# Attention softmax: the second map's scaling moved from VectorE to GpSimd, and 32 small products at the beginning

## The reference, cut to what matters

```python
def gqa_block(qb, k, v):
    s = jnp.einsum('bqhgd,bshd->bhgqs', qb, k).astype(jnp.float32) * (HEAD_DIM ** -0.5)
    p = jax.nn.softmax(s, axis=-1).astype(v.dtype)
    return jnp.einsum('bhgqs,bshd->bqhgd', p, v)

def diff_block(qb, k, v, lam):
    s = jnp.einsum('bqhmd,bshmd->bhmqs', qb, k).astype(jnp.float32) * (HEAD_DIM ** -0.5)
    p = jax.nn.softmax(s, axis=-1)
    a = p[:, :, 0] - lam[None, :, None, None] * p[:, :, 1]
    return jnp.einsum('bhqs,bshe->bqhe', a.astype(v.dtype), v)

def trunk_layer(x, mod, g_attn, g_ffn, mix_w, moe_w, rope, ctx, lam_init):
    shift1, scale1, gate1, shift2, scale2, gate2 = jnp.split(mod, 6, axis=-1)
    h = rms_norm(x, g_attn) * (1.0 + scale1) + shift1
    m, own_ctx = token_mixing(h, mix_w, rope, ctx, lam_init)
    x = x + gate1 * m
    h = rms_norm(x, g_ffn) * (1.0 + scale2) + shift2
    x = x + gate2 * expert_choice_ffn(h, *moe_w)
    return x, own_ctx
```

## Time and profile before

| | us |
|---|---|
| median of 3 runs (1146.23 to 1149.08) | 1146.9 |
| the profiled execution | 1145.81 |
| its span, first to last instruction | 1144.0 |
| TensorE busy (share of the span) | 1097.6 (96%) |
| VectorE busy | 528.1 (46%) |
| ScalarE busy | 363.2 (32%) |
| GpSimd busy | 132.4 (12%) |

### The profile page before, as it was taken

One profiled execution on the slowest core, in us unless ns is written; L12 is line 12 of the kernel. 1 busy time (PEld: TensorE's weight loads), 2 busy tenths in 40 slices (PEclk: granted clock), 3 DMA queues, 4 the chain that ended last, 5 costly groups with the idle time before them and its releaser, 6 DMA issues.

```text
span 1144.0 us, 28118 instructions
## 1 busy us (share of the span) xinstructions
PE 1097.6 (96%) x12524; PEld 828.2 (72%) x12524; DVE 528.1 (46%) x961; ACT 363.2 (32%) x846; POOL 132.4 (12%) x173
## 2 busy tenths in 40 slices
PE   6999999999999999999998999999999999999993
PEld 4679875666677777777877877777777777777761
DVE  4574538879958142334976033332233223333235
ACT  4333327778753223022163221222222222211103
POOL 2332300000000000002012111111110111110021
PEclk9999999999999999999999999999999999999997
DMA  9932242111031545359987999999999999999993
GB/s 359 299 107 68 77 84 63 35 31 41 1 109 38 184 147 147 106 190 300 355 303 320 402 398 406 407 405 409 414 406 405 408 404 408 405 408 405 410 321 143
DMA packets 86747, 295.32 MB, mean 258 GB/s; under 512 B 27249, under 2 KB 28530, under 8 KB 62050
## 3 DMA queue, kind: packets, MB, share of 16 engines
q1 hardware_dynamic: 79104, 269.77, 61.5%
q0 software_dynamic: 6528, 20.10, 6.1%
q10 hardware_dynamic: 994, 3.65, 0.9%
HBM read 273.25 MB, written 15.00 MB: 252 GB/s over the span
## 4 chain that ended last, share of the span: by engine, by line
PE 85%; DMA 7%; issue 2%; ACT 2%; DVE 2%; SPq 1%; POOLq 0%; POOL 0%; ACTq 0%; DVEq 0%
PE ps L1207 39%; PE ps L772 10%; PE ps L774 9%; PE ps L773 9%; PE ps L994 4%; PE ps L1013 3%; PE ps L1032 2%; PE ps L1036 2%; DMA x_dram<-y_row,rows_t 2%; DMA x_dram<-xn_p 1%; DMA raw_first<-in_w_in_dram 1%; DMA x_f<-x_dram 1%; PE ps L794 1%; DMA raw<-in_w_in_dram 1%; PE ps L978 1%
## 5 line engine op out<-in xcount | busy, mean ns | idle before, releaser
L2124 DVE SCALAR_TENSOR_TENSOR y_row<-ps,gates,gate_q 32x256 f32<-32x256 f32 (+1 forms) x184 | 88.3, 480 | 238.5 <-PE ps L1207 236.0
L1564 ACT ACTIVATE h_t<-ps 128x256 f32<-128x256 f32 x48 | 15.0, 384 | 374.7 <-PE ps L1207 374.7
L772 PE MATMUL ps<-w_hi,ht 128*128 128x512 f32 (+1 forms) x320 | 124.2, 388 | 0.6 <-DVE q_n L1728 0.6
L774 PE MATMUL ps<-w_hi,ht 128*128 128x512 f32 (+1 forms) x320 | 121.8, 381 | 0.0
L773 PE MATMUL ps<-raw_lo,ht 128*128 128x512 f32 (+1 forms) x320 | 121.7, 380 | 0.0
L1207 PE MATMUL ps<-late,xe 128*32 128x256 f32 x1824 | 103.6, 379 | 0.0
L537 DVE TENSOR_TENSOR raw_lo<-raw,w_hi 128x1024 fp32r<-128x1024 f32 x48 | 58.2, 1234 | 78.9 <-ACT w_hi L532 78.2
L1207 PEld LDWEIGHTS ps<-late,xe 128*32 128x32 f32 x1824 | 77.0, 110 | 23.3
L1207 PE MATMUL ps<-raw,xe 128*32 128x256 f32 x1392 | 88.1, 379 | 0.9 <-issue 0.8
L532 ACT ACTIVATE w_hi<-raw 128x1024 fp32r<-128x1024 f32 x48 | 48.7, 1053 | 123.6 <-DMA raw<-in_w_in_dram 68.1
L2354 POOL DMA_INDIRECT xg<-x_dram,rows x48 | 46.1, 961 | 320.7 <-PE ps L1207 293.2
(11 more groups left out here) (315 smaller groups left out, 1831.0 us busy)
## 6 DMA issues: line engine op xcount, KB each, us to landing
late<-in_w_exp_down_dram SPq DMA_DIRECT2D x25, 1024.0 KB, 20.4
late<-in_w_exp_up_dram SPq DMA_DIRECT2D x21, 1024.0 KB, 28.8
late<-in_w_exp_gate_dram SPq DMA_DIRECT2D x17, 1024.0 KB, 24.7
raw<-in_w_in_dram SPq DMA_DIRECT2D x16, 1024.0 KB, 5.5
raw<-in_w_exp_gate_dram SPq DMA_DIRECT2D x16, 1024.0 KB
raw_gate<-in_w_exp_up_dram SPq DMA_DIRECT2D x14, 1024.0 KB
raw<-in_w_exp_up_dram SPq DMA_DIRECT2D x13, 1024.0 KB
raw_gate<-in_w_exp_down_dram SPq DMA_DIRECT2D x13, 1024.0 KB
```

The lines of the kernel that those rows point to most:

```text
L772: pe.matmul(b, stat_hi(k, tt), hi[:, kk, :], start=first, stop=False)
L774: mm = pe.matmul(b, stat_lo(k, tt), hi[:, kk, :], start=False, stop=last)
L2124: return dve.scalar_tensor_tensor(y_row[n % 2][32 * v:32 * v + count, 256 * q:256 * q + 256], bank(b, o, o + 256, src), gates[src, n % EG, ...
```

## The change

VectorE no longer scales the second map. GpSimd does this for all 40 units, in a loop of its own behind its last transfer for the input projection (`pool.tensor_scalar`, 40 instructions): in a plain unit by the reciprocal and by a column of ones, in a differential unit by the reciprocal and by lambda. It waits for the reciprocal (`s_inv`) and signals `s_second`. VectorE's first-map scaling of plain units stays behind the reciprocal; the merge of differential units (`combine`) now waits for `s_second`, and stands between the two row maxima. TensorE's transposes of a plain unit wait for `s_second` too, as soon as they reach the second map.

At the beginning TensorE gets 32 throw-away calls between the first `spin(8)` and `turn_tokens(0)`: rows 32a to 32a+31 of the identity as weights of 64 columns, over 128 columns, into four PSUM banks.

```diff
--- before.py
+++ after.py
@@ -425,7 +425,7 @@
         s_kc = sem("s_kc"); s_kpair = sem("s_kpair"); s_vc = sem("s_vc"); s_vac = sem("s_vac")
         s_qt = sem("s_qt")
         s_sc = sem("s_sc"); s_max = sem("s_max"); s_exp = sem("s_exp"); 
-        s_nrm = sem("s_nrm"); s_c1 = sem("s_c1"); s_comb = sem("s_comb"); s_ptr = sem("s_ptr")
+        s_nrm = sem("s_nrm"); s_inv = sem("s_inv"); s_second = sem("s_second"); s_comb = sem("s_comb"); s_ptr = sem("s_ptr")
         s_ph = sem("s_ph"); s_pl = sem("s_pl"); s_pv = sem("s_pv"); s_oev = sem("s_oev");
         s_ysq = sem("s_ysq"); s_yms = sem("s_yms"); s_yn = sem("s_yn")
         s_yh = sem("s_yh"); s_yl = sem("s_yl")
@@ -870,6 +870,11 @@
 
             part_chunk(0, 0)
             spin(8)
+            for n in range(4):
+                for a in range(4):
+                    for v in range(2):
+                        pe.matmul(bank(1 + a, 0, P, slice(64 * v, 64 * v + 64)), ident[32 * a:32 * a + 32, 64 * v:64 * v + 64],
+                                  ident[32 * a:32 * a + 32, :], start=True, stop=True)
             turn_tokens(0)
             turn_tokens(1)
             spin(8)
@@ -1006,7 +1011,9 @@
                     if p >= PLAIN:
                         pe.wait_ge(s_comb, i - PLAIN * NT + 1)
                     else:
-                        pe.wait_ge(s_nrm, 2 * i + tiles[-1] // per + 1)
+                        pe.wait_ge(s_nrm, i + 1)
+                        if tiles[-1] >= per:
+                            pe.wait_ge(s_second, i + 1)
                     piece_bank_free(n)
                     for b, x in enumerate(tiles):
                         kt = x % per
@@ -1805,22 +1812,22 @@
             def inverse_sums(i):
                 o = 2 * i % 8
                 dve.wait_ge(s_exp, 2 * i + 2)
-                dve.reciprocal(row_inv[:, o:o + 2], row_sum[:, o:o + 2]).then_inc(s_dve, 1)
-                own()
-
-            def normalise(i):
+                dve.reciprocal(row_inv[:, o:o + 2], row_sum[:, o:o + 2]).then_inc(s_inv, 1)
+
+            def normalise_first(i):
+                p, t = PUS[i]
+                cols, o = KTL * P if t < NTL else P, 2 * i % 8
+                a = prob_row(2 * i)[:, 0:cols]
+                if p < PLAIN:
+                    dve.wait_ge(s_inv, i + 1)
+                    dve.tensor_scalar(a, a, row_inv[:, o:o + 1], None, ALU.mult).then_inc(s_nrm, 1)
+
+            def combine(i):
                 p, t = PUS[i]
                 cols, o = KTL * P if t < NTL else P, 2 * i % 8
                 a, b = prob_row(2 * i)[:, 0:cols], prob_row(2 * i + 1)[:, 0:cols]
-                dve.wait_ge(s_dve, own(0))
-                if p < PLAIN:
-                    dve.tensor_scalar(a, a, row_inv[:, o:o + 1], None, ALU.mult).then_inc(s_nrm, 1)
-                    dve.tensor_scalar(b, b, row_inv[:, o + 1:o + 2], None, ALU.mult).then_inc(s_nrm, 1)
-                else:
-                    g = 2 * HB + p - PLAIN
-                    dve.tensor_scalar(b, b, row_inv[:, o + 1:o + 2], lam[:, g:g + 1], ALU.mult, ALU.mult)\
-                       .then_inc(s_c1, 1)
-                    dve.wait_ge(s_c1, i - PLAIN * NT + 1)
+                if p >= PLAIN:
+                    dve.wait_ge(s_second, i + 1)
                     dve.scalar_tensor_tensor(a, a, row_inv[:, o:o + 1], b, ALU.mult, ALU.subtract).then_inc(s_comb, 1)
 
             def probs_turned(i):
@@ -1838,11 +1845,14 @@
             for i in range(SLOTS):
                 if 1 <= i <= len(PUS):
                     inverse_sums(i - 1)
-                    normalise(i - 1)
+                    normalise_first(i - 1)
                 if 0 <= i - LAG < len(PUS) and i not in QUERY_SLOTS:
                     probs_turned(i - LAG)
                 if i + 1 < len(PUS):
                     row_max(2 * i + 2)
+                if 1 <= i <= len(PUS):
+                    combine(i - 1)
+                if i + 1 < len(PUS):
                     row_max(2 * i + 3)
                 if 0 <= i - LAG < len(PUS) and i in QUERY_SLOTS:
                     probs_turned(i - LAG)
@@ -2295,6 +2305,17 @@
             pool.wait_ge(s_free_a, 3 * NT)
             pool.dma_start(new_diff_v[0, 0].rearrange("p h d -> p (h d)"), vb_n[:, 2 + NTL, :]).then_inc(s_out, 16)
 
+            for i, (p, t) in enumerate(PUS):
+                cols, o = KTL * P if t < NTL else P, 2 * i % 8
+                b = prob_row(2 * i + 1)[:, 0:cols]
+                g = 2 * HB + p - PLAIN
+                pool.wait_ge(s_inv, i + 1)
+                if p < PLAIN:
+                    pool.tensor_scalar(b, b, row_inv[:, o + 1:o + 2], one, ALU.mult, ALU.mult).then_inc(s_second, 1)
+                else:
+                    pool.tensor_scalar(b, b, row_inv[:, o + 1:o + 2], lam[:, g:g + 1], ALU.mult, ALU.mult)\
+                        .then_inc(s_second, 1)
+
             pool.wait_ge(s_kout, 32)
 
             pool.wait_ge(s_half, gemm_half(11, 3) + 1)
```

## The result

| | before | changed |
|---|---|---|
| median, us (6 runs each) | 1146.9 | 1152.4 (1151.4 to 1153.7) |
| ratio to before (95%) | | 1.0046 (1.0036 to 1.0056) |
| the profiled execution, us | 1145.81 | 1152.75 |
| its span | 1144.0 | 1150.9 |
| TensorE, VectorE, GpSimd busy, us | 1097.6, 528.1, 132.4 | 1102.3, 506.0, 175.5 |

The change costs 5.5 us by the medians. The forecast was 6.7. VectorE is relieved of 22 us, GpSimd is given 43, and TensorE shows 5 us more although it computes the same but for the 32 small calls at the beginning (1.2 us): the rest is products spread out by waits. Lines have moved by 5 to 7 (L994 is now L999, L998 L1003, L1013 L1020, L1036 L1043, L1801 L1808, L1824 L1831, L1416 L1423).

The account below looks back on a forecast made before the run. TensorE was taken as the bound; late merges and row maxima in four differential heads cost 1.3, 1.85, 1.85 and 1.7, together 6.7 us, all else 0: 1146.9 + 6.7 = 1153.6 us, range 1147.5 to 1160.

Parts of the forecast that it names:

- VectorE's saving is worth 0: Taking the second map's scaling off VectorE gains 0 us, since TensorE waited for none of these scalings.
- 0.52 us of slack, 0.47 late: Differential slots: 0.52 us of slack hides the second map's softmax; the moved merge makes its PSUM bank 0.47 us late.
- larger slack: Rival: the slack is larger than thought and only context slots pay, 1149 us; 0.18 together with a missed cover.
- 0.15 in the slot with query turns: Second differential slot with query turns: TensorE has more to do (3.97 us), so only 0.15 us of lateness is left.
- 1.2 us at the context tile: Differential half, A being a slot's first score product start: late merge delays the next full slot 1.2 us per head.
- The last head, 1.7: Last differential head, whose slots have no query turns and end in the tail: taken to lose 1.7 us.
- d, the time of a GpSimd scaling: GpSimd's time for 768 columns in a differential slot: taken as 0.95 us, bounded by 0.80 and 1.45.
- The quarrel over ports: VectorE and GpSimd at SBUF: GpSimd waits some 0.5 us in plain slots, covered by the spare slot; cost 0 us.
- The products, 0: Throw-away products at the beginning: 1.0 to 2.6 us, hidden by TensorE's 2.75 us idle time before 50.69; cost 0 us.
- VectorE the real bound: Rival: VectorE's 3.63 us of work a slot bounds the differential half, so the change gains, 1142 us; chance 0.08.
- Slow GpSimd: Rival: from d = 1.7 every merge waits for GpSimd; 1163 us at d = 2.4; 0.12 together with clock falls.
- The clock falls: Rival: new TensorE waits, largest 1.2 us, lower the clock; four falls give 1159 us; 0.12 together with slow GpSimd.

Follow-up runs that it names:

- plain_only: Kernel before, with GpSimd scaling the second map in the 20 plain units alone, old order, no throw-away products: 1146.76 us, ratio 0.9996.
- early_inverse: Changed kernel without throw-away products, merge ahead of both row maxima, reciprocal one slot earlier in the differential half: 1146.33 us, ratio 0.9993.
- split_merge: Kernel before, with only the merge's last third (256 of 768 columns) and the short merges between the row maxima: 1148.61 us, ratio 1.0018.
- early_double: early_inverse with GpSimd scaling each differential unit in two instructions, by the reciprocal and then by lambda: 1147.14 us, ratio 0.9999.
- order_only: Kernel before, with the merge between the two row maxima in the differential half, VectorE still scaling, no throw-away products: 1151.25 us, ratio 1.0040.
- merge_first: Changed kernel without throw-away products, merge ahead of both row maxima, reciprocal left where it was: 1148.89 us, ratio 1.0018.

## Why the prediction came out as it did

The direction and the mechanism held, the size was 6.7 us where 5.5 was measured. Here are the steps of the forecast, one by one:

- **VectorE's saving is worth 0.** Right: plain_only 0.9996, early_inverse 0.9993, the latter with 20 us less work on VectorE (507.9 instead of 528.1).
- **0.52 us of slack, 0.47 late.** Right. The second scores start 1.09 instead of 0.75 behind the first at 271.77, and the two slots are 0.51 longer together. In split_merge the slack takes a delay of 0.40 us at no cost. The rival *larger slack* falls by the wait at 271.77, where the exponent is waited for. Of the 0.51, 0.06 fall in the first of the two slots and 0.45 in the second.
- **0.15 in the slot with query turns.** It doesn't show where I put it: 274.77 to 278.73 is 3.96, as before (3.97). The lateness is there (the product of 278.73 is 1.74 long), but TensorE's next work doesn't pay for it separately; it is swallowed by the wait at the context tile. This term should have been 0.
- **1.2 us at the context tile.** 1.06 measured. The order of the steps was right, and most were a little too long: the reciprocal starts at A + 3.63 (282.36, forecast 3.70), GpSimd at A + 3.89 (4.01), with 0.98 us of its own (0.95), the merge at A + 4.90 (5.02) and the next full slot 0.86 behind its end. The forecast did not see how the cause divides: 0.88 of it comes from the order even without GpSimd, 0.18 from GpSimd.
- **The last head, 1.7.** 1.11 measured (299.26 to 315.77 before, 304.04 to 321.66 now, up to the first product of L1046, now L1053). This is the term I had not worked out but taken. The kernel before already waits there, which fits its having less to lose, though no run tests this: its score products at 305.99 take 1.71 instead of 1.56 us, its context products at 313.41 take 1.07 instead of 0.91, and the first product behind them waits 0.17 for an exponent.
- **The sum.** 0.98 + 1.56 + 1.57 + 1.11 = 5.2 against 1.3 + 1.85 + 1.85 + 1.7 = 6.7. Of the 1.5 too many, 0.6 is the last head and 0.3 each of the others; in a full head that is the query slot's 0.15 and 0.17 at the context tile, less 0.04 that the two slots before cost more.
- **d, the time of a GpSimd scaling.** 0.98 in a differential unit, inside the bounds and near the copy's end of them. The Trainium skill's (GPSIMD Engine Reference, § 4.1 Engine selection) "roughly line-rate" for one input fits that loosely: VectorE takes 0.68 for the same instruction. The estimate of 1.7 us from the two-input figure in § 3.1 Elementwise doesn't fit.
- **The quarrel over ports.** In a plain slot GpSimd's scaling of the same 768 columns takes 1.41 us instead of 0.98. It started 0.06 behind VectorE's, which took 0.62. The column of ones is not the reason: with it and VectorE elsewhere the instruction takes 0.98 to 0.99 (early_double). The rows of one plain slot:

```profile
215.17 0.62 DVE L1823 TENSOR_SCALAR probs<-probs,row_inv 128x768 f32<-128x768 f32 x1
215.23 1.41 POOL L2314 TENSOR_SCALAR probs<-probs,row_inv,tab 128x768 f32<-128x768 f32 x1 [3.85 <-DVE row_inv L1815]
```

  I had expected some 0.5 of waiting, and that it is harmless; plain_only shows both. The beginning shows the other side. Where GpSimd's copy started first, VectorE's subtraction took 1.73 us (changed kernel, 48.91 and 49.58) or 1.74; in order_only VectorE started first (48.52 and 48.84) and took 1.22. That is the Trainium skill's rule (SBUF — State Buffer, § Who interferes with whom) that the first to start keeps the shared ports, and the traces agree.
- **The products, 0.** Their 1.21 us was within the bounds of 1.0 to 2.6. The first product behind the idle time starts at 51.37 instead of 50.69, but the weight chunk that it waits for has landed 0.67 later too (46.58 instead of 45.91), and the idle time is 2.89 us, longer than the 2.75 of the earlier trace rows: TensorE stood waiting at that point all the same. The clock stayed at 1.00 behind that idle time and had fallen to 0.53 in the kernel before, which is one more reason why two single profiles don't give the price.
- **VectorE the real bound.** Not in this change. The 3.63 us of VectorE's work a slot were a real warning, though: with 0.3 us more on top (merge_first) VectorE is the bound.
- **Slow GpSimd.** It didn't happen, and my price for it was wrong. I had given 1163 at d = 2.4, with 4 of the 9.8 us by ordinary slots; 1162 was reached at 2.06, through the context tile and the clock alone. Nor did every merge wait from 1.7 on: at 2.06 GpSimd held up 8 of 20 merges, and TensorE's products waited for 4.
- **The clock falls.** Not in this change: the granted clock is 1.00 in every stretch from 170 to 338 us, and TensorE's longest new wait in the attention is 0.41 us. The 1.2 us that I had taken as the largest new wait come in pieces, the two longest of 0.40 and 0.21 us (283.62 and 284.71).

## What to carry to other kernels

Before an operation is moved to an idle engine, follow the *result* through the queues that it must now pass: here the price came from the place of one 1 us instruction between two that TensorE needs, and not from the slower engine. Work out the slack of each buffer that comes free from one slot's starts (0.52 us here, of a 3.64 us slot). A delay inside it cost nothing here (0.40), one beyond it about the excess (0.51 for a delay of 0.94), and the slots followed by short ones have the least. If work is to be handed to another engine all the same, start its first step as early as its inputs are there (the reciprocal, one slot earlier). With that, even a doubled GpSimd time cost nothing that could be measured.

## What the runs showed of the hardware

- A GpSimd scaling with two per-row scalars takes 0.98 us for 128x768 float32 and 0.45 for 128x128, which makes an estimate of 0.83 ns a column with 0.34 us fixed. It starts 0.26 us after the start of the reciprocal that releases it (282.36 to 282.62).
- A second dependent GpSimd instruction starts 1.08 us after the first of 0.98: 0.10 us between them (early_double, 282.25 and 283.33).
- 64 instructions of 32x64 tiles over 128 columns took 1.21 us together, where 16 of the router's took 0.64.
- The granted clock fell to 0.50 after TensorE had stood 0.3 to 0.7 and then 1.3 us, in four of four places, and after about 1.0 us in three of four. In the changed kernel the 2.89 us ahead of 51.37 were followed by a clock of 1.00, where the 2.75 us before were followed by 0.53. At this place near 50 us the traces of all thirteen kernels can be set side by side: the four waits of 0.90 to 1.66 us had no fall behind them, and of the nine from 1.81 to 3.13 us all but the changed kernel's had one. In the context slots the clock fell behind waits of 0.97 to 1.30 us. The length of one wait doesn't say by itself whether the clock falls.
